# A second set of score buffers for the local attention, and earlier loads for the output projection

## The reference, cut to what matters

```python
proj = xn @ w_in[l]
q_a, k_a, v_a, qkv_g, z_g, a_g, b_g = jnp.split(proj, SPLIT_POINTS, axis=-1)
attn = _windowed_gqa(q_a, k_a, v_a, band_bias, in_window, attn_sink[l])   # (..., reshapes left out)
gdn = _gdn_mixer(qkv_g, z_g, a_g, b_g, conv_w[l], gdn_a_log[l], gdn_dt_bias[l], gdn_norm_w[l])
h = h + jnp.concatenate([attn, gdn], axis=-1) @ w_out[l]
hn = _rmsnorm(h, norm_ffn_w[l])
h = h + jnp.square(jax.nn.relu(hn @ w_ffn_in[l])) @ w_ffn_out[l]

# _windowed_gqa, for each block of 128 queries against its three key blocks
scores = q @ k^T * 64**-0.5 + bias            # 8 heads, 128 x 384
probs = softmax(concat([scores, sink]))[..., :-1]
out = probs @ v
```

## Time and profile before

| | |
|---|---|
| median of 3 runs | 2545.34 us |
| the profiled execution | 2549.41 us |
| its span, first to last instruction | 2547.6 us |
| busy in the span | PE 94%, PE weight loads 75%, DVE 56%, ACT 41%, POOL 41% |
| granted TensorE clock, mean | 0.971 of full speed |

### The profile page before, as it was taken

The page is one execution under the profiler, slowest core; times in us unless marked ns, Lnnn a source line. Parts: engine busy times, 40 slices in busy tenths (PEclk is TensorE's granted clock), DMA queues, the critical chain, the costliest instruction groups (busy, mean ns, idle before and its releaser), DMA issues. The chain is left out here.

```text
span 2547.6 us, 31180 instructions
## 1 busy us (share of the span) xinstructions
PE 2398.1 (94%) x11797; PEld 1912.8 (75%) x11797; DVE 1420.9 (56%) x1866; ACT 1031.9 (41%) x1748; POOL 1039.3 (41%) x647
## 2 busy tenths in 40 slices
PE   8999799988596999999999999999999999999986
PEld 6778688776384888878788777777777788877765
DVE  7754165543349555576848657676646541114763
ACT  5661234445225555544446334344334331115532
POOL 2212156452227666655777422212122252216653
PEclk9999999999698999999999999999999999999998
DMA  4113221111422444394544411211111352236562
GB/s 167 42 58 106 91 62 45 41 30 55 153 91 75 158 156 161 129 312 142 174 139 130 141 34 50 79 50 55 67 50 50 127 200 95 95 113 206 166 209 80
DMA packets 141730, 279.12 MB, mean 110 GB/s; under 512 B 26595, under 2 KB 36067, under 8 KB 141580
## 3 DMA queue, kind: packets, MB, share of 16 engines
q1 hardware_dynamic: 141580, 277.12, 32.9%
HBM read 200.44 MB, written 76.63 MB: 109 GB/s over the span
## 5 line engine op out<-in xcount | busy, mean ns | idle before, releaser
L1793 POOL TENSOR_TENSOR t<-t,t 128x512 fp32r<-128x512 f32 (+1 forms) x431 | 741.3, 1726 | 1174.7 <-ACT t L858 1154.7
L550 PE MATMUL bank<-t,t 128*128 128x512 f32 x1840 | 744.1, 404 | 32.3 <-ACT t L858 27.8
L554 PE MATMUL bank<-t,t 128*128 128x512 f32 x1840 | 725.7, 394 | 5.8 <-DVE t L1230 5.0
L552 PE MATMUL bank<-t,t 128*128 128x512 f32 x1840 | 725.1, 394 | 6.1 <-POOL t L1793 5.9
L858 ACT ACTIVATE t<-t 128x512 fp32r<-128x512 f32 (+1 forms) x581 | 398.8, 708 | 778.3 <-PE bank L554 388.4
L550 PEld LDWEIGHTS bank<-t,t 128*128 128x128 f32 x1840 | 349.8, 190 | 114.6 <-issue 41.2
L554 PEld LDWEIGHTS bank<-t,t 128*128 128x128 f32 x1840 | 349.0, 190 | 85.6 <-DVE t L1230 9.8
L552 PEld LDWEIGHTS bank<-t,t 128*128 128x128 f32 x1840 | 350.1, 190 | 84.1 <-POOL t L1793 11.5
L752 PE MATMUL bank<-t,t 128*128 128x512 f32 x896 | 352.4, 393 | 19.6 <-ACT t L858 18.8
L756 PE MATMUL bank<-t,t 128*128 128x512 f32 x896 | 352.7, 394 | 7.1 <-DVE t L1230 4.3
L754 PE MATMUL bank<-t,t 128*128 128x512 f32 x896 | 351.5, 392 | 1.9 <-POOL t L1793 1.9
(11 more groups left out here) (213 smaller groups left out, 2501.3 us busy)
## 6 DMA issues: line engine op xcount, KB each, us to landing
t<-in_w SPq DMA_DIRECT2D x87, 512.0 KB, 3.7
hid_scr<-t SPq DMA_DIRECT2D x112, 256.0 KB, 2.3
t<-hid_scr SPq DMA_DIRECT2D x112, 256.0 KB, 2.8
t<-in_wf SPq DMA_DIRECT2D x80, 256.0 KB, 3.8
g_scr<-t SPq DMA_DIRECT2D x36, 512.0 KB, 2.6
t<-g_scr SPq DMA_DIRECT2D x72, 256.0 KB, 3.3
t<-in_wf SPq DMA_DIRECT2D x35, 512.0 KB, 4.4
t<-in_wo SPq DMA_DIRECT2D x24, 512.0 KB, 3.7
```

Of the source, the lines that this page charges most:

```text
L550: e.matmul(ps[:, :], hi[:, w, :], XH[:, x, hs], start=k == 0, stop=False)
L552: e.matmul(ps[:, :], lo[:, w, :], XH[:, x, hs], start=False, stop=False)
L554: last = e.matmul(ps[:, :], hi[:, w, :], XL[:, x, hs], start=False, stop=k == j.nk - 1)
L1793: return e.tensor_tensor(out, x, high.bitcast(F32), ALU.subtract)
```

## The change

P2: `prob` and `sm` are doubled (the second `prob` at 208 to 220 KB, the second `sm` at 220 KB); block n uses set n % 2, `am` of block n waits for block n-2, and the planner's `behind` goes to n-2. P3: `ya` and `zl` wait for `sc(0, 7)` and `sc(1, 7)` (and `ya` for the store of its own four blocks) in place of `p2_end`; the casts `yah` and `zh` wait for `p2_x`, which has `atr(7, 1)` in place of `aout(7)`. `wpair(0, r)`, whose place is now used by the second `prob`, waits for `atr(7, 1)`.

```diff
-        self.bias, self.prob = many(84, 6, 2, [128, 4, 384]), many(96, 6, 2, [128, 4, 384])
+        self.bias, self.prob = many(84, 6, 2, [128, 4, 384]), [many(96, 6, 2, [128, 4, 384]), many(208, 6, 2, [128, 4, 384])]
-        self.sm, self.sqg = at(11.25, [128, 2, 64]), at(9, [128, 4, 128])
+        self.sm, self.sqg = [at(11.25, [128, 2, 64]), at(220, [128, 2, 64])], at(9, [128, 4, 128])
...
     def yah(h, j):
-        q.wait_ge(done("ya", h, j))
+        q.wait_ge(done("ya", h, j), *[done(*x) for x in K.p2_x])
     def zh(h, j):
-        q.wait_ge(done("zm", h, j), *[done(*x) for x in K.p2_end])
+        q.wait_ge(done("zm", h, j), *[done(*x) for x in K.p2_x])
...
     def am(g, n, j):
-        if n:
-            q.wait_ge(done("atr", n - 1, K.blocks(n - 1) - 1), done("ap", g, n - 1), done("ae", g, n - 1))
-        e.tensor_tensor_reduce(out=M.prob[g][:, j, 0:w], ...
+        if n >= 2:
+            q.wait_ge(done("atr", n - 2, K.blocks(n - 2) - 1), done("ap", g, n - 2), done("ae", g, n - 2))
+        e.tensor_tensor_reduce(out=M.prob[n % 2][g][:, j, 0:w], ...
...
     def wpair(i, r):
-        if i == 1:
+        if i == 0:
+            q.wait_ge(done("atr", 7, 1))
+        elif i == 1:
...
     def ya(h, j):
-        q.wait_ge(*[done("aout", 4 * h + 3)], *[done(*y) for y in K.p2_end])
+        q.wait_ge(done("aout", 4 * h + 3), done("sc", 0, 7), done("sc", 1, 7))
     def zl(h, j):
-        q.wait_ge(done("z_out", j), *[done(*y) for y in K.p2_end])
+        q.wait_ge(done("z_out", j), done("sc", 0, 7), done("sc", 1, 7))
...
         self.p2_end = [("co", 0, 7), ("co", 1, 7), ("aout", 7)]
+        self.p2_x = [("co", 0, 7), ("co", 1, 7), ("atr", 7, 1)]
...
-        before = [("atr", (n - 1, K.blocks(n - 1) - 1))] if n else []
+        before = [("atr", (n - 2, K.blocks(n - 2) - 1))] if n >= 2 else []
```

More of the change, by code:

```diff
@@ L728, in atr @@
             for j in range(4):
-                last = e.transpose(banks[5 + g][:, 128 * j:128 * j + 128], M.prob[g][:, j, 128 * s:128 * s + 128], ident)
+                last = e.transpose(banks[5 + g][:, 128 * j:128 * j + 128], M.prob[n % 2][g][:, j, 128 * s:128 * s + 128], ident)
         last.then_inc(*tick("atr", n, s))
@@ L1033, in ae @@
     def ae(g, n):
-        w, sm, prob = 128 * (min(n + 2, 8) - max(n - 1, 0)), M.sm[:, g, :], M.prob[g]
+        w, sm, prob = 128 * (min(n + 2, 8) - max(n - 1, 0)), M.sm[n % 2][:, g, :], M.prob[n % 2][g]
         q.wait_ge(done("as1", n))
@@ L1392, in am @@
         q.wait_ge(done("aqk", n, j), done("abias", g))
-        if n:
-            q.wait_ge(done("atr", n - 1, K.blocks(n - 1) - 1), done("ap", g, n - 1), done("ae", g, n - 1))
-        e.tensor_tensor_reduce(out=M.prob[g][:, j, 0:w], in0=banks[5 + g][:, 0:w], in1=M.bias[g][:, j, b0:b0 + w], scale=1.0, scalar=NEG,
-                               op0=ALU.add, op1=ALU.max, accum_out=M.sm[:, g, j:j + 1]).then_inc(*tick("am", g, n, j))
+        if n >= 2:
+            q.wait_ge(done("atr", n - 2, K.blocks(n - 2) - 1), done("ap", g, n - 2), done("ae", g, n - 2))
+        e.tensor_tensor_reduce(out=M.prob[n % 2][g][:, j, 0:w], in0=banks[5 + g][:, 0:w], in1=M.bias[g][:, j, b0:b0 + w], scale=1.0, scalar=NEG,
+                               op0=ALU.add, op1=ALU.max, accum_out=M.sm[n % 2][:, g, j:j + 1]).then_inc(*tick("am", g, n, j))
     def as1(n):
-        sm, sink = M.sm, M.rows[:, 16:24].rearrange("p (g j) -> p g j", g=2)
+        sm, sink = M.sm[n % 2], M.rows[:, 16:24].rearrange("p (g j) -> p g j", g=2)
         q.wait_ge(*[done("am", g, n, j) for g in range(2) for j in range(4)])
@@ L1407, in as2 @@
     def as2(n):
-        sm = M.sm
+        sm = M.sm[n % 2]
         q.wait_ge(done("ae", 0, n), done("ae", 1, n))
@@ L1847, in ap @@
     def ap(g, n):
-        w, P = 128 * (min(n + 2, 8) - max(n - 1, 0)), M.prob[g]
+        w, P = 128 * (min(n + 2, 8) - max(n - 1, 0)), M.prob[n % 2][g]
         q.wait_ge(done("as2", n), done("ae", g, n))
-        e.tensor_tensor(P[:, :, 0:w], P[:, :, 0:w], M.sm[:, g, 32:36].unsqueeze(2).broadcast_to([128, 4, w]), ALU.mult).then_inc(*tick("ap", g, n))
+        e.tensor_tensor(P[:, :, 0:w], P[:, :, 0:w], M.sm[n % 2][:, g, 32:36].unsqueeze(2).broadcast_to([128, 4, w]), ALU.mult).then_inc(*tick("ap", g, n))
     def zlo(h, j):
@@ L1972, in wpair @@
     def wpair(i, r):
-        if i == 1:
+        if i == 0:
+            q.wait_ge(done("atr", 7, 1))
+        elif i == 1:
             q.wait_ge(*[done(x, K.turn[1 - r, t]) for t in (0, 2) for x in ("vh", "vl")])
-        elif i:
+        else:
             q.wait_ge(*[done(x, K.turn[i - 2, t]) for t in range(7) if i - 2 >= EARLY or t not in (0, 2) for x in ("vh", "vl")])
```

## The result

| | before | after |
|---|---|---|
| median of the runs | 2545.39 us | 2508.88 us (2507.24 to 2513.38) |
| ratio, with its 95% interval | | 0.9855 [0.9843, 0.9867] |
| the profiled execution, its span | 2549.41, 2547.6 us | 2507.24, 2505.4 us |
| granted TensorE clock, mean | 0.971 | 0.978 |

The change made the kernel 36.5 us faster; 2512 us (-33.8) was predicted. The size is right, and the sum is not: three of its terms were too small, and one that was not in it took a good part back.

The account below looks back on a forecast made before the run. PE bounds P2's middle, and the serial attention chain its end, before a hole ahead of P3. Terms -13 - 11.0 - 8.3 - 1.5 = -33.8 us took the median 2545.3 to 2512 us; range 2495 to 2533 (8 in 10).

Parts of the forecast that it names:

- (a): P2's attention with two score sets: blocks start earlier, -8 us in the tail and -5 in the middle, -13 in all.
- (c): P3's first four jobs: fewer transfers after the last store, fourth job 31.4 us after T, -8.3 us.
- (d): Kernel start: `wpair(0)` and `ws(0)` move later, hidden in the stretch from 701.6; -1.5 us, bounds 0 and -2.6.
- T: End of DVE's last attention copy out (last `ao`) in P2: forecast at 638 plus or minus 5 instead of 650.9.
- (b): Hole between T and P3's first matmul: store landing, load and cast leave the path, -11.0 of 11.5 us.
- the 9 us bound: Lower gain of -9 us for the hole, if DVE's `gg`, waiting for the store, stood ahead of the first low parts.
- (e): Everything after the fourth job (701.6): keeps its length and moves as a whole, plus or minus 3 us.
- R1: Rival: P2 doesn't end earlier, the other savings of -20.8 us stay; 2525 us, chance 0.20.
- R2: Rival: much more room in P2, hidden in PE's busy time, and full-speed first four jobs; -47.5 us, 2498, chance 0.06.
- R3: Rival: second half's operands queue behind the residual and P2 grows by some 10 us; about -2 us, 2543, chance 0.09.
- R4: Rival: in P2, two blocks' exponentials back to back on ACT delay the delta rule's copies; +8 us, 2553, chance 0.08.

Follow-up runs that it names:

- experiment 1: The changed kernel, but with P3's loads and casts (`ya`, `zl`, `yah`, `zh`) waiting as in the kernel before: 2520.82 us, 0.9892 of the kernel before.
- experiment 3: The kernel before, with only `wpair(0)` made to wait for `atr(7, 1)`: 2541.74 us, 0.9979 of the kernel before.
- experiment 4: The changed kernel, but blocks 1 to 6 wait for the block before; only block 7 uses the second score set's freedom: 2519.99 us, 0.9899 of the kernel before.
- Experiment 6: The changed kernel, with block 7's last copies (`atc`, `ao`) ranked ahead of P3's casts and low parts: 2506.94 us, 0.984 of the kernel before.
- experiment 5: The changed kernel, with the second half's operand loads (`zl`, `ya`) put behind the residual's loads on SP: 2517.35 us, 0.9878 of the kernel before.

## Why the prediction was right in size, step by step

That the total came within 3 us is partly luck. In the profiled executions (a), (c) and (d) were together some 19 us larger than forecast (22.5, 15.6 and 3.9 us, for 13, 8.3 and 1.5), and a delay of 11.9 us that was not in the sum took most of that back; the rest of the difference lies between the profiled executions and the medians.

*(a) Two score sets: -13 predicted, some -22 by experiments 1 and 3.* The mechanism is the one forecast, in both places; by experiment 4, 8 to 11 us lie in the middle, where I had 5, and 11 to 14 in the tail, where I had 8. In the middle I filled only a part of PE's waits for ACT's copies. The waits of PE in the changed kernel, 348 to 611 us, show that all six pieces of the earlier trace rows are gone and what is left:

```profile
PE bank L710 <- ACT t L1025: 3.9, 1, 3.9
PE bank L700 <- ACT t L858: 2.6, 1, 2.6
PE bank L721 <- DVE t L1395: 2.3, 2, 1.2
PE bank L620 <- DVE t L1376: 0.5, 1, 0.5
```

And I held PE's busy time fixed at 291.8 us. It isn't: the granted clock of the middle is 0.99 where it was 0.97, and the same matmuls take less. The group of the 1248 matmuls of L620 (columns: busy us, mean ns, idle before) went from 167.3 us and 288 ns, with 23.2 us of idle before it, to this, on the page of the changed kernel:

```profile
L620 PE MATMUL bank<-t,t 128*128 128x128 f32 x1248 | 161.2, 280 | 11.3 <-DVE t L1330 9.2
```

A part of the gain is thus in "busy" time that I had put down as work. How the 22 us divide is seen in the windows of experiment 1, cut like the first two of the earlier trace rows:

```profile
324.00:603.00 279.00, 270.09 (x2093) 228.19 (x2093) 155.73 (x362) 135.97 (x368) 135.44 (x97) 0.99 0.14 43
603.00:624.10 21.10, 12.77 (x44) 6.30 (x44) 4.54 (x6) 9.52 (x22) 9.44 (x5) 0.64 0.36 123
```

PE's idle in these two is 8.9 + 8.3 = 17.2 us in place of 35.1. The first scores run at 320.1 here, ahead of the window; cut from the first scores to T in both kernels (320.08 to 624.12, and 324.39 to 650.91), with 2161 matmul records in each, PE's idle is 17.7 us in place of 35.1, 17.4 less, where I had 13, and its busy time is 286.3 in place of 291.4, 5.1 less, where I had none. 17.4 + 5.1 = 22.5. That the clock rose because the waits went is read from the two going together; no run changes one without the other.

*The missing term: +11.9 us on T.* I asked of every moved step what it releases, and not what it now stands in front of. With one line for `wpair(0)` I named the queue behind it on SP; for the casts on ACT and for `zm`, `ws(0)` and the low parts on DVE I didn't. The casts now wait for `atr(7, 1)`, exactly the moment at which the last copies become ready as well, and the planner placed them first. Between 636.0 and 624.1 lie 4.2 us of the casts (5.40 less 1.18) and some 7 us of DVE work ahead of the last `ao`. Experiment 6, which puts the copies first, has T at 622.9 and so shows it. From this and the too small (a) the forecast T of 638 came out near the 636.0 that was seen, by two errors that cancel. My list of what would show (a) had T, and T passed; it was experiment 1 that parted the two.

*(b) The hole: -11.0 predicted, -11.35 in the profile.* Right. The casts are out of the path and the first matmul comes 0.1 us after T. `gg` waits for the store at 638.33 on DVE, as feared for the 9 us bound, but with no low part queued behind it that was needed then.

*(c) The first four jobs: -8.3 predicted, -15.6 in the profile.* Two steps of it failed. The first is "6.5 MB follow the store", with the residual ahead of the second half's operands. The z of the second half went before the store and `ya` ahead of the residual, and the fourth job came 23.9 us after T instead of 31.4. Where my order does hold, in experiment 5, the transfers end some 23 us after T, near the 22 that I forecast, and the third job waits 5.30 us for them; but after that wait the matmuls run at a granted clock of 0.50 again and wait for low parts, and the fourth job comes at 35.6.

The second is "the transfers are the limit" as an account of the 17.4 us of excess before the change. From the first matmul to the fourth job (662.36 to 701.72) PE was busy 32.4 us and idle 7.0; 1.96 us of the idle was the third job's wait for an operand, and 5.0 us were waits for DVE's low parts. In the changed kernel the same stretch (636.10 to 659.91) has 23.8 us busy and no idle. So of the 15.6 us, 7.0 are waits, and 8.6 are matmuls that ran slower, at a granted clock of 0.71 for the stretch against 0.92. I had named the clock as a cause and given it no price. Four jobs at full clock are 21.8 us, so little is left here.

The rule of the Trainium skill ("SBUF — State Buffer", "Who interferes with whom"), that a DVE instruction with two SBUF inputs and a GpSimd instruction that reads SBUF contend, agrees with the trace. The four L1230 from 622.09 take 1.59 us each beside POOL's low parts, and L1560 and L1562 take 1.75 and 1.74 beside the next ones, where L1429 at 628.98, with POOL idle, took 0.68. POOL in the changed kernel:

```profile
621.61 6.29 POOL L1793 TENSOR_TENSOR t<-t,t 128x512 fp32r<-128x512 f32 x4 [7.96 <-ACT t L858]
630.39 3.26 POOL L1793 TENSOR_TENSOR t<-t,t 128x512 fp32r<-128x512 f32 x2 [2.49 <-ACT t L858]
```

The slowing did not land on the first job, where I had looked for it, since the low parts were done before T. Some 2 of the 7 us of DVE work ahead of the last `ao` are that slowing (twice 1.75 against 0.68).

*(d) The weights: -1.5 predicted, -5.3 [-7.6, -2.8] measured alone.* Too small, outside my bounds of 0 and -2.6; the mechanism is the one forecast. The wait of L567 fell from 2.30 us at 42.58 to this, in the changed kernel:

```profile
39.74 1.13 PE L567 MATMUL bank<-t,t 128*128 128x512 f32 x2 [0.54 <-DVE t L1221]
```

2.8 us came by there, where I had counted only the wait shown. The 1 MB that the second half of x no longer stands behind is a likely cause (those loads are issued at 4.36 for 6.44); no run separates it from the four DVE instructions. Behind the wait a little more came: before the change the next matmuls, from 44.3 to 46.6, ran at a granted clock of 0.50, and in the changed kernel those from 40.93 are at full clock. The other side of (d), that `ws(0)` would come after T and be hidden in the stretch from 701.6, was wrong: it ran at 628 to 634, ahead of the last `ao`.

*(e)* -0.4 us: right.

*The rivals.* R1 (P2 doesn't end earlier) falls with experiment 1. R2 had more truth than its 0.06: for the middle (-11) and the four jobs (-16) it came nearer than my forecast did. The rule of the Trainium skill that it leaned on ("Perfetto Trace Analysis", "Identifying the Most-Contended Engine": weight-load time is the better measure) gave 68 us of room in P2; 22 came, and the weight-load share of the middle only rose from 78% to 80% (230.82 of 287.6), so as a size it was not borne out. But it points the right way, since some us did lie in matmul busy time. R3 (given back) has the load order of experiments 5 and 6, not that of the change, and P2 did not grow. R4 (exponentials back to back) did not occur: PE's waits for L858 in P2's middle fell from 14.1 us (12.6 of them L620's) to 2.6. One slip in the bounds: R1's 2525 is 8 us below the range's end of 2533, not 6.

## What to carry to other kernels

When a wait is relaxed, ask which older step becomes ready at that same moment on the same engine, and who goes first; a step that "waits for the same event" as the last copies of the stage before is a rival of theirs. When the end of one stage moves, follow the buffers on: here an earlier T kept the buffers of the next loads busy for longer relative to it, and 10 of 13 us went back until the residual was moved as well. And test a forecast by its parts, since an intermediate time that comes out right can be the sum of two errors.

## What was not expected of the hardware

In these traces idle gaps went together with a lower granted clock, so they cost twice. In P2's middle the idle fell by 8.9 us (22.05 to 13.2), the granted clock went from 0.97 to 0.99, and 1248 equal matmuls took 280 ns in place of 288. The same shows at the border. In the changed kernel P3 starts after 7.94 us without a matmul, at a granted clock of 0.50 (the 1.2 GHz level), its matmuls issued 0.43 us apart; with no wait between them they run at the full 2.4 GHz from 639.65 on. In experiment 1 they start at 634.83 after 11.45 us without one, also at 0.50, meet waits for low parts of 1.14 and 0.57 us, and stay at that level until 646.35 (timelines of PE, the changed kernel and then experiment 1):

```profile
639.65 0.46 PE L554 MATMUL bank<-t,t 128*128 128x512 f32 x1
```

```profile
637.16 0.79 PE L554 MATMUL bank<-t,t 128*128 128x512 f32 x1 [1.14 <-DVE t L1230]
646.35 0.44 PE L554 MATMUL bank<-t,t 128*128 128x512 f32 x1
```

So the early low parts probably bought clock as well as their own waits. That slower matmuls make up 8.6 of the 15.6 us of (c) is measured; how much of the clock is owed to the low parts, how much to the shorter stretch without work before P3, and how much to the third job's operands, no run here separates.
